# One mean product for the sum of squares before six stages of a two-block network kernel

## The chip, the cores and the metric

The kernel runs on one core of a Trainium2 chip. The metric is the device time of one execution in microseconds (us). Below, TensorE (PE in profile rows) multiplies matrices, VectorE (DVE) and ScalarE (ACT) work on tiles elementwise, and SyncE (SP) issues the loads. Each engine takes its instructions in the order in which the program wrote them and waits on semaphores for the others.

## The reference

A hybrid block of two layers is followed by a mixer block of one layer, on 512 tokens of width 1024, all in float32. Cut to what matters here, the norms and what stands on both sides of them:

```
def layer_norm(x, g, b):
    mu = xf.mean(-1);  var = square(xf - mu).mean(-1)
    return (xf - mu) * rsqrt(var + LN_EPS) * g + b
def rmsnorm(x, g):
    return x * rsqrt(mean(x * x, -1) + RMS_EPS) * g

# hybrid_layer, twice:
h = layer_norm(ALPHA * x + 0.5 * swiglu(x, ffn1_w_gu, ffn1_w_down), ...)
... = split(h @ w_in);  merged = gated sum of three branches
h = layer_norm(ALPHA * h + merged @ w_out, ...)
x = layer_norm(ALPHA * h + 0.5 * swiglu(h, ffn2_w_gu, ffn2_w_down), ...)
# second block, once:
x = x + token_mixer(rmsnorm(x, norm_mix_g), w_in, ..., w_out)
x = x + conv_ffn(rmsnorm(x, norm_ffn_g), w_up, ..., w_down)
return rmsnorm(x, norm_final_g)
```

Every `@` reduces over 1024 or more inputs, and every norm needs a mean of squares over the 1024 channels of each token.

## The kernel before, in words

**Tiles.** An activation is kept transposed: eight tiles of 128 channels by 512 tokens, R[0] to R[7] for the residual. Each matrix product is made of blocks of 128 by 128 weights. To hold float32 accuracy, a block is three products: the rounded weights by the rounded operand (L1982), the rounded weights by its rest (L1983), the rest of the weights by the rounded operand (L1991). Four blocks of weights arrive as one slab by DMA; ScalarE rounds the slab (L2253, `w_hi`) and VectorE makes its rest (L2606, `w_lo`).

**How a stage ends.** `update` makes the eight output tiles of `ffn1_down`, `w_out`, `ffn2_down` or their like in the second block. After tile m, VectorE adds it to the residual (`add_up`, L2624). ScalarE squares the tile (L2284, writes a page of SBUF), VectorE adds the squares of tiles up to m - 1 to a running total (`squares_add`, L2658), and in the layer norms it adds the tile itself to a running sum for the mean (L2671). A mean over channels, which lie on partitions, is a product with a 128 by 128 matrix whose entries are all 1/1024. It is a product in float32 of 128 by 512, which the trace shows as two records.

**How the next stage begins.** A norm's factors are known only once tile 7 is added up. So that TensorE needn't wait, the next stage begins its first products from the residual without its norm (class `Early`, in the text "early products"): ScalarE multiplies tile m by the gain and rounds it (L2332), VectorE makes the rest (L2682), and TensorE multiplies the eight tiles in their order; in layer norms it also multiplies the gains and offsets by the same weights (L1989, L1990, four columns wide). The norm is put right afterwards on the outputs. An `Early` has a `count` of such outputs: 2, except before the second block's mixer, where `EarlyTwice` has 4.

**The order around the change.** The order on each engine is set by one planner, which runs the program once with estimated times (`Pace`) and again identically for each engine. `stats.ended()` is where the norm of tile 7 is asked for: `behind(7)` is called there, behind the early part of tile 7 (L2332, L2682) and behind the early products of tiles 0 to 6 that the planner put ahead. `behind(7)` takes the total of the squares of tiles 0 to 6 and the squares of tile 7 apart: TensorE multiplies the first by the mean matrix (L2004), waits for the second, and adds its product to the same bank (L2007). In the layer norms one more product follows for the mean (`mean_matmul`, L1999), and then the square of the mean, the variance, its logarithm and an exponential (L2308, L2722, L2292, L2295). The products of tile 7 for the next stage come next on TensorE. In the second block's RMS norm there is no product for the mean.

`behind(7)` with L2004 and L2007 runs eight times: before the stages after `ffn1_down`, `w_out`, `ffn2_down` of layer 0, the same of layer 1, after `w_out_2`, and before the last norm.

Of the kernel before, what the change touches and what calls it, by code (L numbers as in the profile page):

```python
# [1596 lines left out]
class Squares:  # L1597
# [28 lines left out]
    def behind(self, m):  # L1626
        o, k = self.o, self.k
        while self.sq:
            t, q, squared = self.sq.pop(0)
            if not self.summed:  # L1630
                k.will(tensor="var")
                o.mean_matmul(k, self.v, q.f[:, :], self.first, t == 7, [squared])
                o.pages.give(q, k["var"])
            elif self.first:
                self.sum, k["sum"] = q, squared
            elif t < 7:
                before = k["sum"]
                k.will(vector="sum")
                o.squares_add(k, self.sum, q, before, squared)
                o.pages.give(q, k["sum"])  # L1640
            else:
                k.will(tensor="most var")
                o.mean_of_two(k, self.v, self.sum, q, squared)
                o.pages.give(self.sum, k["most"])
                o.pages.give(q, k["var"])
            self.first = False
# [1608 lines left out]
```

## Time and profile before

| | us |
|---|---|
| Median of 3 runs | 3683.18 |
| Lowest and highest run | 3682.66, 3684.90 |
| The profiled execution, its own time | 3684.97 |
| Its span, first to last instruction | 3683.2 |
| TensorE busy in it | 3628.9 |
| VectorE busy in it | 1978.8 |
| ScalarE busy in it | 1525.7 |

The page has the busy time of each engine, the span in 40 slices with the granted clock of TensorE, the chain of work that ended last, and groups of instructions. The busy time of TensorE says only that it seldom waits; what an edit is worth is read from the timeline at the place of the edit, where the start of each instruction, its duration and, in brackets, the idle time before it stand.

### The profile page before, as it was taken

To read this page: it belongs to the slowest core of one execution; us is meant where nothing else is said; L and a number is where in the kernel's file an instruction comes from. 1 tells how busy PE (TensorE), PEld (TensorE's weight loads), DVE (VectorE), ACT (ScalarE), POOL (GpSimd) and SP (SyncE) were. 2 spreads that over 40 slices of the span, in tenths; PEclk is the share of its full clock that TensorE was granted. 3 is DMA by queue.
4 is the path that set the end of the run, shared out by engine and by line. 5 is a ranking of instruction groups with operands and counts; after the bars stand their busy time and mean duration, and the time that the engine had idled before them with its cause. 6 is when DMAs were issued, how large, how long until landed. Compare 5 with 4: busy or idle time off the path is not lost.

```text
span 3683.2 us, 44504 instructions
## 1 busy us (share of the span) xinstructions
PE 3628.9 (99%) x17166; PEld 2913.6 (79%) x17166; DVE 1978.8 (54%) x3808; ACT 1525.7 (41%) x2928; POOL 0.2 (0%) x4
## 2 busy tenths in 40 slices
PE   9999999999999999999999999999998999999998
PEld 7888878877778888888888877788876677778887
DVE  4433565556753345334665576733346787566643
ACT  4433454454343334333554553533234444344432
POOL 0000000000000000000000000000000000000000
PEclk9999999999999999999999999999998999999999
DMA  4433321112333333333221113233322222233332
GB/s 147 120 112 94 87 86 52 44 47 71 90 87 94 94 95 88 93 94 94 86 66 49 43 56 87 84 94 94 94 72 64 82 65 82 82 89 94 94 94 89
DMA packets 169546, 308.42 MB, mean 84 GB/s; under 512 B 18870, under 2 KB 21079, under 8 KB 169336
## 3 DMA queue, kind: packets, MB, share of 16 engines
q1 hardware_dynamic: 169336, 305.59, 28.6%
q8 instruction: 136, 2.23, 0.3%
q14 instruction: 74, 0.61, 0.1%
HBM read 300.80 MB, written 4.72 MB: 83 GB/s over the span
## 4 chain that ended last, share of the span: by engine, by line
PE 93%; DVE 3%; ACT 2%; issue 1%; DMA 0%; DVEq 0%; SPq 0%; ACTq 0%
PE bank L1991 27%; PE bank L1982 27%; PE bank L1983 27%; PE bank L1965 3%; PE bank L2024 1%; PE bank L1970 1%; PE bank L1999 1%; PE bank L2044 1%; DVE w_lo L2606 1%; PE bank L2065 0%; PE bank L2199 0%; PE bank L2037 0%; PE bank L1990 0%; PE bank L2207 0%; DVE page_f L2677 0%
## 5 line engine op out<-in xcount | busy, mean ns | idle before, releaser
L1982 PE MATMUL bank<-page_r,w_hi 128*128 128x512 f32 (+1 forms) x4488 | 1803.3, 402 | 19.7 <-DVE w_lo L2606 11.3
L1991 PE MATMUL bank<-page_r,w_lo 128*128 128x512 f32 (+1 forms) x4488 | 1776.3, 396 | 0.0
L1983 PE MATMUL bank<-page_r,w_hi 128*128 128x512 f32 (+1 forms) x4488 | 1766.8, 394 | 0.0
L2253 ACT ACTIVATE w_hi<-raw 128x512 fp32r<-128x512 f32 x1122 | 699.0, 627 | 1024.4 <-PE bank L1991 1021.1
L1982 PEld LDWEIGHTS bank<-page_r,w_hi 128*128 128x128 f32 x4488 | 848.1, 189 | 225.6 <-issue 18.2
L1983 PEld LDWEIGHTS bank<-page_r,w_hi 128*128 128x128 f32 x4488 | 847.6, 189 | 192.2 <-issue 6.9
L1991 PEld LDWEIGHTS bank<-page_r,w_lo 128*128 128x128 f32 x4488 | 847.6, 189 | 192.1
L2606 DVE TENSOR_TENSOR w_lo<-raw,w_hi 128x512 fp32r<-128x512 f32 x1122 | 747.3, 687 | 438.4 <-ACT w_hi L2253 436.6
L2746 DVE TENSOR_TENSOR page_f<-page_f,bank 128x512 f32<-128x512 f32 x88 | 60.5, 688 | 321.8 <-PE bank L1991 275.3
L1965 PEld LDWEIGHTS bank<-page_f 128*128 128x128 f32 x1344 | 161.6, 192 | 9.1 <-issue 1.9
L1965 PE MATMUL bank<-page_f 128*128 128x128 f32 x1344 | 163.3, 276 | 0.4 <-DVE page_f L2940 0.4
L2624 DVE SCALAR_TENSOR_TENSOR page_f<-bank,page_f 128x512 f32<-128x512 f32 x64 | 44.2, 690 | 164.2 <-PE bank L1991 163.6
L2327 ACT ACTIVATE page_r<-page_f 128x512 fp32r<-128x512 f32 x88 | 55.6, 632 | 176.3 <-DVE page_f L2746 176.3
L2284 ACT ACTIVATE page_f<-page_f 128x512 f32<-128x512 f32 (+1 forms) x80 | 48.5, 611 | 147.2 <-DVE page_f L2624 131.1
L3074 DVE SCALAR_TENSOR_TENSOR page_f<-bank,par,page_f 128x511 f32<-128x511 f32 x88 | 65.4, 748 | 60.1 <-ACT page_f L2567 58.5
L2749 DVE TENSOR_TENSOR page_r<-page_f,page_r 128x512 fp32r<-128x512 f32 x88 | 60.9, 693 | 64.0 <-ACT page_r L2327 64.0
L2370 ACT ACTIVATE page_f<-bank 128x256 f32<-128x256 f32 (+3 forms) x144 | 50.2, 388 | 104.5 <-PE bank L1970 102.6
L1970 PE MATMUL bank<-cst,page_f 128*128 128x128 f32 x452 | 72.1, 277 | 4.9 <-DVE page_f L2898 2.9
L2360 ACT ACTIVATE page_f<-bank 128x512 f32<-128x512 f32 x80 | 47.7, 597 | 69.5 <-PE bank L1991 69.4
L2754 DVE SCALAR_TENSOR_TENSOR page_f<-page_f,bank 128x512 f32<-128x512 f32 x80 | 54.7, 685 | 39.0 <-PE bank L1991 38.7
L1970 PEld LDWEIGHTS bank<-cst,page_f 128*128 128x128 f32 x452 | 53.5, 141 | 25.3 <-issue 7.0
L2822 DVE SCALAR_TENSOR_TENSOR page_f<-bank,par,page_f 128x511 f32<-128x511 f32 (+2 forms) x72 | 53.8, 748 | 34.5 <-ACT page_f L2412 32.8
(235 smaller groups left out, 2394.5 us busy)
## 6 DMA issues: line engine op xcount, KB each, us to landing
raw<-weights SPq DMA_DIRECT2D x1122, 256.0 KB, 2.6
page_f<-x_t SPq DMA_DIRECT2D x8, 256.0 KB, 5.4
bias_rows<-page_f SPq DMA_DIRECT2D x8, 256.0 KB, 2.0
page_f<-bias_rows SPq DMA_DIRECT2D x8, 256.0 KB, 3.3
out_t<-page_f SPq DMA_DIRECT2D x8, 256.0 KB, 2.1
cst<-consts SPq DMA_DIRECT2D x4, 272.0 KB, 4.2
page_f<-mem_t SPq DMA_DIRECT2D x8, 128.0 KB, 3.3
bias_rows<-page_f SPq DMA_DIRECT2D x8, 64.0 KB, 1.9
```

What stands on the lines that cost most here:

```text
L1965: last = self.e.matmul(b.tile(i), x, y, start=True, stop=True)
L1970: last = self.e.transpose(b.tile(i), ap[:, i * P:(i + 1) * P], self.const("ident"))
L1982: self.e.matmul(o, hi, X.hi[kt], start=first, stop=False)
L1983: self.e.matmul(o, hi, X.lo[kt], start=False, stop=False)
L1991: last = self.e.matmul(o, lo, X.hi[kt], start=False, stop=final)
L2253: self.e.activation(self.m.w_hi[:, s % NHI, :], self.m.raw[:, s % NRAW, :], ACT.Copy) \
L2327: self.e.activation(h.r[:, :], s.f[:, :], ACT.Copy).then_inc(k.lane.scalar, 1)
L2606: self.e.tensor_tensor(self.m.w_lo[:, s % NRAW, :], self.m.raw[:, s % NRAW, :], self.m.w_hi[:, s % NHI, :].bitcast(F32), ALU.subtract).the ...
L2746: self.e.tensor_tensor(s.f[:, :], s.f[:, :], lift.f[:, :], ALU.mult).then_inc(k.lane.vector, 1)
L2749: self.e.tensor_tensor(l.r[:, :], s.f[:, :], h.r[:, :].bitcast(F32), ALU.subtract).then_inc(k.lane.vector, 1)
L2754: self.e.scalar_tensor_tensor(out=g.f[:, :], in0=g.f[:, :], scalar=1.0, in1=b.f[:, :], op0=ALU.add, op1=ALU.mult).then_inc(k.lane.vector, 1)
L3074: self.e.scalar_tensor_tensor(out=p.f[:, sh:], in0=b.f[:, 0:SEQ - sh], scalar=self.col("conv2", (2 - sh) * 2 * FT + m), in1=p.f[:, sh:], o ...
```

## The change

At the last tile, where the stage has an `Early` of two products, VectorE adds the squares of tile 7 to the total as well, and TensorE makes the mean with one product instead of two. The order in which two pages go back to the stock changes with it.

```
@@ Squares.behind
                 k.will(vector="sum")
                 o.squares_add(k, self.sum, q, before, squared)
                 o.pages.give(q, k["sum"])
+            elif self.early and self.early.count == 2:
+                before = k["sum"]
+                k.will(vector="sum", tensor="var")
+                o.squares_add(k, self.sum, q, before, squared)
+                o.mean_matmul(k, self.v, self.sum.f[:, :], True, True, [k["sum"]])
+                o.pages.give(q, k["sum"])
+                o.pages.give(self.sum, k["var"])
             else:
                 k.will(tensor="most var")
                 o.mean_of_two(k, self.v, self.sum, q, squared)
```

Six of the eight places have a count of 2: `ffn1_down`, `w_out` and `ffn2_down` of layer 0, `ffn1_down` and `w_out` of layer 1, and `w_out_2`. The one before the second block's mixer (a count of 4) and the last norm (no early products) stay. In all, TensorE has six products fewer and VectorE six additions more; ScalarE and SyncE have the same instructions in the same order. Lines of the changed kernel stand seven further down, so L2004 and L2007 give way to L2006, L2658 is L2665 and L2682 is L2689.

TensorE after `w_out` of layer 0, before the change (`cst` is the mean matrix, `page_f` squares or the sum of tiles, `page_r` and `w_hi` or `w_lo` an operand and weights):

```order
L1991 MATMUL bank<-page_r,w_lo 128x512
L2004 MATMUL bank<-page_f,cst 128x512 [waits norm_vector]
L2007 MATMUL bank<-page_f,cst 128x512 [waits norm_scalar]
L1999 MATMUL bank<-page_f,cst 128x512 [waits norm_vector]
L1982 MATMUL bank<-page_r,w_hi 128x512 [waits early_vector]
L1983 MATMUL bank<-page_r,w_hi 128x512
```

and with the change:

```order
L1998 MATMUL bank<-page_r,w_lo 128x512
L2006 MATMUL bank<-page_f,cst 128x512 [waits norm_vector]
L2006 MATMUL bank<-page_f,cst 128x512
L1989 MATMUL bank<-page_r,w_hi 128x512 [waits early_vector]
L1990 MATMUL bank<-page_r,w_hi 128x512
```

The product with the total that waited for the squares of tiles 0 to 6 and the one that waited for ScalarE's squares of tile 7 have become one, which waits for VectorE's new sum; the second L2006 is the product for the mean.

VectorE at the same place, before the change, from the addition of tile 7 on:

```order
L2624 SCALAR_TENSOR_TENSOR page_f<-bank,page_f 128x512 [waits norm_vector,blocks_multiplied]
L2671 TENSOR_TENSOR page_f<-page_f 128x512 [waits norm_vector]
L2682 SCALAR_TENSOR_TENSOR page_r<-page_f,par,page_r 128x512 [waits early_scalar]
L2722 TENSOR_TENSOR page_f<-bank,page_f 128x512 [waits norm_scalar,norm_tensor]
L2689 SCALAR_TENSOR_TENSOR page_f<-bank,page_f 128x512 [waits norm_scalar,norm_tensor,merge_vector]
```

and with the change:

```order
L2631 SCALAR_TENSOR_TENSOR page_f<-bank,page_f 128x512 [waits norm_vector,blocks_multiplied]
L2678 TENSOR_TENSOR page_f<-page_f 128x512 [waits norm_vector]
L2689 SCALAR_TENSOR_TENSOR page_r<-page_f,par,page_r 128x512 [waits early_scalar]
L2665 TENSOR_TENSOR page_f<-page_f 128x512 [waits norm_scalar]
L2729 TENSOR_TENSOR page_f<-bank,page_f 128x512 [waits norm_scalar,norm_tensor]
L2696 SCALAR_TENSOR_TENSOR page_f<-bank,page_f 128x512 [waits norm_scalar,norm_tensor,merge_vector]
```

The new addition (L2665) stands behind the rest of tile 7 (L2689, before L2682), which itself waits for ScalarE's rounding. At the other four places with a layer norm the rows are the same; after `w_out_2` the new addition stands between the rest of tile 7 and a slab's rest.

## Rows read from the trace of the kernel before

**Rows 1.** The page: busy times, granted clock in 40 slices, chain by engine.

```profile
PE 3628.9 (99%) x17166; PEld 2913.6 (79%) x17166; DVE 1978.8 (54%) x3808; ACT 1525.7 (41%) x2928; POOL 0.2 (0%) x4
PEclk9999999999999999999999999999998999999999
PE 93%; DVE 3%; ACT 2%; issue 1%; DMA 0%; DVEq 0%; SPq 0%; ACTq 0%
```

**Rows 2.** Timeline (start, duration, engine, line) after `ffn1_down` of layer 0.

```profile
431.61 0.63 ACT L2284 ACTIVATE page_f<-page_f 128x512 f32<-128x512 f32 x1 [2.83 <-DVE page_f L2624]
...
432.89 0.75 DVE L2682 SCALAR_TENSOR_TENSOR page_r<-page_f,par,page_r 128x512 fp32r<-128x512 f32 x1 [0.59 <-ACT page_r L2332]
...
433.44 1.02 PE L2004 MATMUL bank<-page_f,cst 128*128 128x512 f32 x2
...
435.15 1.02 PE L1999 MATMUL bank<-page_f,cst 128*128 128x512 f32 x2
...
436.25 0.40 PE L1983 MATMUL bank<-page_r,w_hi 128*128 128x512 f32 x1
...
436.91 0.69 DVE L2722 TENSOR_TENSOR page_f<-bank,page_f 128x512 f32<-128x512 f32 x1 [3.27 <-ACT page_f L2308]
```

**Rows 3.** The same after `ffn2_down` of layer 0.

```profile
1389.12 0.75 DVE L2682 SCALAR_TENSOR_TENSOR page_r<-page_f,par,page_r 128x512 fp32r<-128x512 f32 x1 [0.66 <-ACT page_r L2332]
...
1392.41 0.40 PE L1983 MATMUL bank<-page_r,w_hi 128*128 128x512 f32 x1
```

**Rows 4.** The same after `w_out` of layer 0.

```profile
1011.35 0.48 PE L1991 MATMUL bank<-page_r,w_lo 128*128 128x512 f32 x1
1011.76 0.69 DVE L2658 TENSOR_TENSOR page_f<-page_f 128x512 f32<-128x512 f32 x1
...
1012.50 1.13 PE L2004 MATMUL bank<-page_f,cst 128*128 128x512 f32 x2 [0.67 <-DVE page_f L2658]
...
1013.76 1.13 PE L2007 MATMUL bank<-page_f,cst 128*128 128x512 f32 x2
...
1014.36 0.75 DVE L2682 SCALAR_TENSOR_TENSOR page_r<-page_f,par,page_r 128x512 fp32r<-128x512 f32 x1 [0.58 <-ACT page_r L2332]
...
1014.73 1.02 PE L1999 MATMUL bank<-page_f,cst 128*128 128x512 f32 x2
...
1015.82 0.40 PE L1983 MATMUL bank<-page_r,w_hi 128*128 128x512 f32 x1
```

**Rows 5.** The same after `w_out_2`.

```profile
3301.92 0.75 DVE L2682 SCALAR_TENSOR_TENSOR page_r<-page_f,par,page_r 128x512 fp32r<-128x512 f32 x1 [1.31 <-ACT page_r L2332]
3302.59 0.69 DVE L2606 TENSOR_TENSOR w_lo<-raw,w_hi 128x512 fp32r<-128x512 f32 x1
...
3303.77 0.40 PE L1983 MATMUL bank<-page_r,w_hi 128*128 128x512 f32 x1
```

**Rows 6.** TensorE's timeline where it resumes after a wait (idle before in brackets).

```profile
662.49 3.35 PE L2065 MATMUL bank<-page_f,cst 128*128 128x512 f32 x4 [1.97 <-DVE page_f L2882]
...
666.07 0.54 PE L1983 MATMUL bank<-page_r,w_hi 128*128 128x512 f32 x1
...
1995.17 1.99 PE L2065 MATMUL bank<-page_f,cst 128*128 128x512 f32 x4 [1.99 <-DVE page_f L2882]
...
1997.22 0.40 PE L1983 MATMUL bank<-page_r,w_hi 128*128 128x512 f32 x1
...
2731.46 3.65 PE L1999 MATMUL bank<-page_f,cst 128*128 128x512 f32 x4 [3.56 <-ACT page_f L2284]
...
2767.27 0.77 PE L1982 MATMUL bank<-page_r,w_hi 128*128 128x512 f32 x1 [4.91 <-DVE page_r L2741]
```

**Rows 7.** TensorE by stretches: stretch, its length, busy (count), granted clock, DMA share, GB/s.

```profile
1016.00:1050.00 34.00, 34.00 (x160) 1.00 0.29 86
2730.00:2735.00 5.00, 3.54 (x5) 0.66 0.01 4
2765.00:2770.00 5.00, 2.73 (x7) 0.56 0.00 0
```

## The prediction

> **What bounds the kernel now.** I read the page first. TensorE is busy for 3628.9 of 3683.2 us, and the chain that ended last runs through it for 93% of the span [rows 1]. So what an edit is worth is what it does to TensorE's own sequence: a product taken away is a gain if TensorE isn't made to wait in its place, and work on VectorE (54% busy) costs nothing unless TensorE waits for its result. Both happen here in the same spot, so the busy shares decide nothing, and I went to the timeline at each of the six places. In each I take as goal the start of L1983 in the block of tile 7, the first ordinary product behind the mean products. The four things to look at are when TensorE reaches the first mean product, when the squares of tile 7 are ready, when VectorE ends the rest of tile 7 (L2682), and when L1983 starts.
>
> The sum is made against the profiled execution, whose span (3683.2 us) is almost equal to the median of the runs (3683.18), so I add the difference to the median.
>
> **What is removed.** One mean product of 128 by 512 in float32, six times. From L2004 to L1999 in rows 2 lie two of them: 435.15 - 433.44 = 1.71 us, so 0.86 us for one. Were nothing to wait, this would be 6 x 0.86 = 5.1 us gained.
>
> **What is added.** One VectorE addition of two 128x512 pages, and TensorE's wait for it. Its duration is that of the same operation on other squares, 0.69 us [rows 4]. Its start is set by its place behind L2682, because its other input is there early: after `ffn1_down` the squares are ready at 431.61 + 0.63 = 432.24, before L2682 even starts at 432.89 [rows 2]. Behind an L2682 the next VectorE instruction starts 3302.59 - 3301.92 = 0.67 us later [rows 5]. From the end of an addition to the product that waited for it are 1012.50 - (1011.76 + 0.69) = 0.05 us [rows 4]. So the one product now starts 0.67 + 0.69 + 0.05 = 1.41 us after the start of L2682. A mean product that TensorE had to wait for takes a little longer to the next: 1014.73 - 1013.76 = 0.97 us instead of 0.86 [rows 4]. From the mean's product L1999 to L1983 are 436.25 - 435.15 = 1.10 us [rows 2]. Thus with a layer norm L1983 starts 0.97 + 1.10 = 2.07 us behind the start of the one product.
>
> **Place by place.**
> - After `ffn1_down` of layer 0: one product at 432.89 + 1.41 = 434.30, L1983 at 436.37 in place of 436.25 [rows 2]: 0.12 us later. TensorE idles from 433.44 to 434.30, which is exactly the product that went away.
> - After `ffn2_down` of layer 0: 1389.12 + 1.41 + 2.07 = 1392.60 against 1392.41 [rows 3]: 0.19 later. `ffn1_down` of layer 1 repeats this pattern, another 0.17 to 0.19.
> - After `w_out` of layer 0: here VectorE is behind, because it still makes slab rests, and TensorE reaches the mean products before tile 7 is even added up. Before the change it uses the time: the total of tiles 0 to 6 is multiplied at 1012.50, tile 7's squares at 1013.76 [rows 4]. With the change it can do neither, and waits for L2682 and the addition: 1014.36 + 1.41 = 1015.77, then L1983 at 1017.84 against 1015.82 [rows 4]: 2.02 later. `w_out` of layer 1 is the same pattern, 2.02 again.
> - After `w_out_2`: no product for the mean, so L1983 comes 1.10 + 0.11 = 1.21 us behind the start of the one product (0.11 being what a product waited for takes longer). 3301.92 + 1.41 + 1.21 = 3304.54 against 3303.77 [rows 5]: 0.77 later.
>
> The sum: 0.12 + 2 x 0.18 + 2 x 2.02 + 0.77 = 5.3 us lost. The factors of the norm hang on the same mean products, so they come later by as much as TensorE does, and TensorE meets them at the same distance as before: nothing is given back and nothing is added. On VectorE the instruction behind the new addition waits for ScalarE and TensorE anyway (L2722 follows only when the mean's product is done), so there it covers nothing up. Only after `w_out_2` a slab's rest is pushed by one addition, and TensorE needs that slab three slabs later; I cost it at nothing, and at 0.7 us if that cover were gone. The swapped pages cost nothing, since ScalarE and SyncE keep their rows.
>
> **The clock.** After `w_out` TensorE will now stand still from 1011.35 + 0.48 = 1011.83 to 1015.77, 3.94 us, where the longest pause before was 0.67 us [rows 4] and the clock was granted in full (a 9 in every slice there, and 1.00 behind it) [rows 1, 7]. What such a pause does shows elsewhere. Behind one of 3.56 us the granted clock fell: 0.66 on average over 2730 to 2735. Behind one of 4.91 us it was 0.56 over 2765 to 2770 [rows 6, 7]. The levels being 1.2 and 2.4 GHz, that is most of each stretch at the lower one. Behind pauses of 2 us it is open: the same instructions took from L2065 to L1983 666.07 - 662.49 = 3.58 us in layer 0 and 1997.22 - 1995.17 = 2.05 in layer 1 [rows 6], so one fall costs 1.53 us and the other pause had none. 3.94 lies between the two long pauses, and I take a fall at both `w_out` places. Price: nothing at the low end; 1.7 us at the high end (the 0.66 over 5 us means 0.34 / 0.5 x 5 = 3.4 us at half the clock, and half of them are lost when all of them fall on work). In the stretch from 2765 on, 0.56 means 4.4 of 5 us at the lower level, while work resumed only at 2767.27: a part fell on the pause and cost nothing. So I take 1.35, between 0.7 and 1.7, twice: 2.7 us.
>
> The Trainium skill, in TensorE: Matmul & The Clock Gate, section "Why this matters for your kernels", says to leave no long idle gaps between bursts of matmuls, since one of them brings the lower clock back. That speaks against this change at the two `w_out` places; by this rule the sum is 8.0 us, and without it 5.3. The two long pauses of this trace agree with it.
>
> **Sum.** 5.3 + 2.7 = 8.0 us slower: 3683.2 + 8.0 = 3691.2 us, or 0.22%.
>
> **Rivals.**
> 1. The clock holds, or falls at one of the two places only. For: the twin pauses of 2 us went both ways. Against: both long ones fell. Time 5.3 to 6.9 us later, 3688.5 to 3690.1. Chance 0.24.
> 2. The loss is partly given back, because TensorE would later have waited for something that keeps its time, such as a weight load or VectorE's backlog. Against: TensorE is busy for all of the 34 us behind the first `w_out` place [rows 7], and the four other layer norm places look alike, so no wait is near that could swallow it. It would leave 0 to 4 us, 3683 to 3687. Chance 0.08.
> 3. Faster: the addition isn't late. If VectorE reaches it as soon as the squares are ready, TensorE doesn't wait at four of the places (all but the `w_out` ones) and keeps 0.86 us at each. It decides at the point where the addition ends before TensorE arrives: at 433.44 it would have to start by 432.70, before L2682 starts [rows 2]. The order puts it behind L2682, so this needs the layers' timing to shift. 3683.2 - 4 x 0.86 = 3679.8 at best if the `w_out` places lost nothing either. Chance 0.04.
> 4. VectorE becomes the bound behind the addition: 0.6 to 0.7 us more in its queue six times delays slab rests and the repair of the early products, up to 4 us on top, 3692 to 3695. Against: VectorE idled 3.27 us before L2722 [rows 2]. Chance 0.08.
>
> That the change doesn't do what it says is excluded by the order of the rows: six products fewer, six additions more, nothing else.
>
> **How the numbers follow.** The forecast (a fall at both places) has 0.56. Its own range is 5.3 + 2 x 0.7 = 6.7 to 5.3 + 2 x 1.7 = 8.7 us, so 3689.9 to 3691.9. The whole range takes in rival 1 and half of rival 4: 3687.2 to 3693.4. About 0.2% (7.4 us) is what a measurement of this kernel can tell from no change. Of the forecast's 0.56, three quarters lie beyond that (0.42), and with rival 4 slower has 0.50; same has 0.14 + 0.24 + 0.08 + half of rival 3, 0.47 together; faster 0.03.
>
> **What would show it.** In the profile after: at the three ffn places the one product L2006 preceded by 0.7 to 0.9 us of idle time, released by VectorE L2665, and L1990 (L1983 before) within 0.3 us of its old distance from the rest of tile 7; at the two `w_out` places 3.5 to 4 us of idle time before L2006, and a granted clock clearly under 1.00 in the 5 us behind; after `w_out_2` a wait for the addition as well. The step that I trust least is the price of the clock. If L2006 has no wait before it at the ffn places, the place of the addition was read wrongly; if the idle time is there and the end doesn't move, the view that nothing is given back is wrong.

## The result, and the profile after

| | before | after |
|---|---|---|
| Median, us | 3684.15 (9 runs) | 3694.45 (9 runs) |
| Lowest and highest run | 3682.66, 3685.19 | 3690.39, 3696.41 |
| Ratio, with its 95% interval | | 1.0026 [1.0016, 1.0035] |
| Profiled execution, its own time | 3684.97 | 3691.1 |
| Its span | 3683.2 | 3689.3 |

The change costs 10.3 us, 0.26%. The sign is the one forecast. The size is above the forecast (8.0 us) and the time is above the range (3693.4). The profiled execution lies near the low end of the runs of the changed kernel (3691.1, where the median is 3694.45), so sums made from its trace come out below the median.

The page of the changed kernel, beside [rows 1]: busy times, granted clock by slices, and the chain by engine.

```profile
PE 3628.6 (98%) x17154; PEld 2910.5 (79%) x17154; DVE 1982.5 (54%) x3814; ACT 1525.9 (41%) x2928; POOL 0.2 (0%) x4
PEclk9999999999999999999999999999998999999999
PE 94%; DVE 3%; ACT 2%; issue 1%; DMA 0%; DVEq 0%; ACTq 0%
```

TensorE has twelve records fewer (six products of two records) and still the same busy time. So what the six products saved, some 5 us, came back as longer products elsewhere, and the longer span is idle time on top. A digit of the clock row shows neither: a slice is 92 us long, and a fall of a few microseconds doesn't change it. The waits of TensorE name the new idle time (what it waited for: us in all, times, longest):

```profile
PE bank L2006 <- DVE page_f L2665: 8.4, 6, 2.4
```

Now the six places. After `ffn1_down` of layer 0, beside [rows 2] (start, duration, engine, line, idle before in brackets):

```profile
432.17 0.75 DVE L2689 SCALAR_TENSOR_TENSOR page_r<-page_f,par,page_r 128x512 fp32r<-128x512 f32 x1 [0.59 <-ACT page_r L2339]
...
432.84 0.68 DVE L2665 TENSOR_TENSOR page_f<-page_f 128x512 f32<-128x512 f32 x1
...
433.58 1.98 PE L2006 MATMUL bank<-page_f,cst 128*128 128x512 f32 x4 [0.70 <-DVE page_f L2665]
...
435.63 0.39 PE L1990 MATMUL bank<-page_r,w_hi 128*128 128x512 f32 x1
```

From the rest of tile 7 (L2689) to the one product are 433.58 - 432.17 = 1.41 us, and from there to L1990 2.05. The prediction had 1.41 and 2.07. After `ffn2_down` of layer 0, beside [rows 3]:

```profile
1390.49 0.75 DVE L2689 SCALAR_TENSOR_TENSOR page_r<-page_f,par,page_r 128x512 fp32r<-128x512 f32 x1 [0.66 <-ACT page_r L2339]
...
1391.90 1.98 PE L2006 MATMUL bank<-page_f,cst 128*128 128x512 f32 x4 [0.77 <-DVE page_f L2665]
1393.95 0.39 PE L1990 MATMUL bank<-page_r,w_hi 128*128 128x512 f32 x1
```

L1990 stands 3.46 us behind L2689, where it was 3.29. After `w_out_2`, beside [rows 5], 3309.91 - 3307.31 = 2.60 us in place of 1.85, so 0.75 lost where 0.77 was predicted:

```profile
3307.31 0.75 DVE L2689 SCALAR_TENSOR_TENSOR page_r<-page_f,par,page_r 128x512 fp32r<-128x512 f32 x1 [1.31 <-ACT page_r L2339]
3307.98 0.68 DVE L2665 TENSOR_TENSOR page_f<-page_f 128x512 f32<-128x512 f32 x1
...
3308.72 1.12 PE L2006 MATMUL bank<-page_f,cst 128*128 128x512 f32 x2 [1.36 <-DVE page_f L2665]
...
3309.91 0.39 PE L1990 MATMUL bank<-page_r,w_hi 128*128 128x512 f32 x1
```

And after `w_out` of layer 0, beside [rows 4]: TensorE and VectorE.

```profile
1010.60 0.48 PE L1998 MATMUL bank<-page_r,w_lo 128*128 128x512 f32 x1
1013.48 3.63 PE L2006 MATMUL bank<-page_f,cst 128*128 128x512 f32 x4 [2.40 <-DVE page_f L2665]
1016.27 1.07 PE L1989 MATMUL bank<-page_r,w_hi 128*128 128x512 f32 x1
1017.18 0.40 PE L1990 MATMUL bank<-page_r,w_hi 128*128 128x512 f32 x1
...
1012.07 0.75 DVE L2689 SCALAR_TENSOR_TENSOR page_r<-page_f,par,page_r 128x512 fp32r<-128x512 f32 x1 [0.58 <-ACT page_r L2339]
1012.74 0.68 DVE L2665 TENSOR_TENSOR page_f<-page_f 128x512 f32<-128x512 f32 x1
```

Two things differ from the prediction here. The pause is 2.40 us, not 3.94. And the two products L2006 take 3.63 us for what took 1.98 at the ffn places: from the one product to L1990 are 3.70 us, not 2.05. The windows say why. TensorE by stretches: stretch, its length, busy (count), granted clock, DMA share, GB/s; the changed kernel:

```profile
990.00:1000.00 10.00, 7.99 (x29) 0.83 0.17 55
1010.00:1025.00 15.00, 12.60 (x55) 0.89 0.15 47
2325.00:2335.00 10.00, 8.00 (x28) 0.83 0.20 54
2345.00:2360.00 15.00, 12.58 (x55) 0.89 0.13 41
```

The clock fell behind the pause at both `w_out` places, as forecast, and also 20 us earlier, behind an old pause of 2.0 us in which TensorE waits for a slab's rest:

```profile
992.50 0.50 PE L1989 MATMUL bank<-page_r,w_hi 128*128 128x512 f32 x1 [2.01 <-DVE w_lo L2613]
992.84 0.54 PE L1990 MATMUL bank<-page_r,w_hi 128*128 128x512 f32 x1
993.18 0.63 PE L1998 MATMUL bank<-page_r,w_lo 128*128 128x512 f32 x1
```

**How I cut the traces.** Two executions of one kernel differ by 1 or 2 us at pauses that the change doesn't touch, so starts in one trace can't be set against starts in another. Distances between two marks can. As marks I take the resumption behind that 2.0 us pause (L1982 before, L1989 after) and VectorE's addition of tile 7 after `ffn2_down` (L2624, L2631). Between them lies one `w_out` place and nothing else of the change. In the kernel before they are

```profile
994.79 0.50 PE L1982 MATMUL bank<-page_r,w_hi 128*128 128x512 f32 x1 [2.01 <-DVE w_lo L2606]
...
1387.05 0.69 DVE L2624 SCALAR_TENSOR_TENSOR page_f<-bank,page_f 128x512 f32<-128x512 f32 x1 [2.98 <-PE bank L1991]
```

and after, from 992.50 above to

```profile
1388.41 0.69 DVE L2631 SCALAR_TENSOR_TENSOR page_f<-bank,page_f 128x512 f32<-128x512 f32 x1 [2.98 <-PE bank L1998]
```

so 392.26 us before and 395.91 after: 3.65 us for this place. Cutting the whole program in this way (marks read from the timelines; 662 and 1995 stand for the product behind two other old pauses of 2 us, L2065 before and L2072 after; 2731 for the product behind the 3.56 us pause):

| stretch | before | after | difference | predicted |
|---|---|---|---|---|
| start to 662 | 662.49 | 661.91 | -0.58 | 0.12 |
| 662 to the pause ahead of `w_out` | 332.30 | 330.59 | -1.71 | |
| `w_out` of layer 0 | 392.26 | 395.91 | +3.65 | 2.02 + 1.35 |
| to 1995 (two ffn places) | 608.12 | 608.44 | +0.32 | 0.36 |
| 1995 to the pause ahead of `w_out` | 330.56 | 330.52 | -0.04 | |
| `w_out` of layer 1 | 392.26 | 395.79 | +3.53 | 2.02 + 1.35 |
| to 2731 | 13.47 | 13.49 | +0.02 | |
| to L1990 after `w_out_2` | 572.31 | 573.26 | +0.95 | 0.77 |
| to the end | 379.4 | 379.4 | 0.0 | |

The first ffn place costs 0.10 us (5.46 us from the addition of tile 7 to L1990, before 5.36). Of the 0.95 in the stretch of `w_out_2`, 0.75 is the place itself, so the six places of the change sum to 0.10 + 3.65 + 0.32 + 3.53 + 0.75 = 8.35 us. The other 0.2 of that stretch is what two changes of the clock leave over: it stayed low for a shorter time behind 2827 (from 2731 to the resumption at 3258.86 are 527.40 us, and 526.26 after), and it fell behind a pause of 1.57 us at 3262.91 (granted 0.83 over 3260 to 3270, where it had been 1.00 behind the same pause). The -1.71 is a fall of the clock behind the pause at 662, which this execution of the kernel before had [rows 6] and this one of the changed kernel had not; executions of both kernels without that fall are met below, so it isn't put down to the change. It is the main reason why the spans differ by 6.1 us only.

### The profile page after: what moved, and what is told of

It is laid out like the page before. It is cut to its first block, busy times and chain, and to the rows that moved or that the text cites. A ratio compares the mean times of both kernels' runs of the same rounds, so it can differ in the third digit from the quotient of the medians.

```text
span 3689.3 us, 44487 instructions
## 1 busy us (share of the span) xinstructions
PE 3628.6 (98%) x17154; PEld 2910.5 (79%) x17154; DVE 1982.5 (54%) x3814; ACT 1525.9 (41%) x2928; POOL 0.2 (0%) x4
## 4 chain that ended last, share of the span: by engine, by line
PE 94%; DVE 3%; ACT 2%; issue 1%; DMA 0%; DVEq 0%; ACTq 0%
PE bank L1989 27%; PE bank L1998 27%; PE bank L1990 27%; PE bank L1972 3%; PE bank L2031 1%; PE bank L1977 1%; PE bank L2006 1%; PE bank L2051 1%; PE bank L2206 0%; PE bank L2072 0%; PE bank L2044 0%; DVE w_lo L2613 0%; ACT page_r L2339 0%; PE bank L1997 0%; PE bank L2214 0%
## 5 line engine op out<-in xcount | busy, mean ns | idle before, releaser
L1989 PE MATMUL bank<-page_r,w_hi 128*128 128x512 f32 (+1 forms) x4488 | 1801.9, 402 | 19.4 <-DVE w_lo L2613 11.0
L1990 PE MATMUL bank<-page_r,w_hi 128*128 128x512 f32 (+1 forms) x4488 | 1765.0, 393 | 0.0
L1989 PEld LDWEIGHTS bank<-page_r,w_hi 128*128 128x128 f32 x4488 | 847.8, 189 | 226.7 <-issue 19.5
L1990 PEld LDWEIGHTS bank<-page_r,w_hi 128*128 128x128 f32 x4488 | 847.3, 189 | 193.7 <-issue 7.0
L2631 DVE SCALAR_TENSOR_TENSOR page_f<-bank,page_f 128x512 f32<-128x512 f32 x64 | 44.2, 691 | 165.4 <-PE bank L1998 164.8
```

The costliest lines, as they stand in the source:

```text
L1989: self.e.matmul(o, hi, X.hi[kt], start=first, stop=False)
L1990: self.e.matmul(o, hi, X.lo[kt], start=False, stop=False)
```

## The experiments

In the diffs, a removed line is one of the changed kernel unless a sentence says otherwise. `self.early.number` is the number of the layer norm, 0 to 5; 1 and 4 are those behind `w_out` of the two layers.

**The change alone at its two kinds of place, once more in full, and with the pause filled.** `again` is the changed kernel. `wout_only` keeps the change at the two `w_out` places, `others_only` at the four others:

```diff
-            elif self.early and self.early.count == 2:
+            elif self.early and self.early.number in (1, 4):                               # wout_only
+            elif self.early and self.early.count == 2 and self.early.number not in (1, 4): # others_only
```

`fill` is the changed kernel with three float32 products of constants ahead of the waiting product at the two `w_out` places. They go to the bank that the mean product then overwrites, so what is computed stays the same.

```diff
             elif self.early and self.early.count == 2:
...
+                if self.early.number in (1, 4):
+                    o.fill(self.v, 3)
...
+    def fill(self, v, n):
+        self.clear(v)
+        for _ in range(n):
+            self.e.matmul(v.cols(SEQ), self.const("mean"), self.m.cst[:, 0:SEQ], start=True, stop=True)
```

> The changed kernel once more, for a second profile. Theory A (the loss is TensorE's longer wait at the two w_out places plus the lower clock that such a pause brings): the runs scatter over several us, since the pause falls differently on the clock each time; a pause of 2.4 to 4.0 us before L2006 at both w_out places, a granted clock under 1.00 behind each. Rival B (the additions push VectorE's later work at all six places): the same time with little scatter, and new waits of TensorE elsewhere. Time 10 us over the kernel before, within 2 us, by both.

> The change at the two w_out places alone, the other four as before. Theory A: nearly all of the loss, 7 to 10 us over the kernel before. Rival B (each addition costs its own length and a slab's delay, wherever it stands): a third of it, about 3.4 us.

> The change at the four other places alone, the two w_out places as before. Theory A: 0.12 + 2 x 0.18 + 0.77 = 1.3 us over the kernel before, and no fall of the clock behind L2006. Rival B: two thirds of the loss, about 7 us.

> The changed kernel with three idle products (mean matrix by constants, 0.86 us each) issued at each w_out place before the product that waits for the addition; their result is overwritten. They change no dependence, they only keep TensorE working for 2.6 us of the pause. Theory A: the clock stays full behind the w_out places and the time is what is left without the clock's part, 5 to 6 us over the kernel before, some 4 to 5 us under the changed kernel. Rival B (the clock doesn't matter, VectorE does): no change against the changed kernel, 10 us.

| | median, us | against before | ratio |
|---|---|---|---|
| again | 3693.01 | +8.8 | 1.0023 [1.0015, 1.0032] |
| wout_only | 3691.92 | +7.7 | 1.0024 [1.0014, 1.0033] |
| others_only | 3683.84 | -0.3 | 1.0000 [0.9991, 1.0009] |
| fill | 3690.28 | +6.1 | 1.0017 [1.0008, 1.0026] |

The loss belongs to the two `w_out` places. At the four others the trace of the changed kernel has 0.70 + 0.77 + 0.75 + 1.36 = 3.6 us of idle time before L2006, against four products of 0.86 saved; what is left, 1.3 us by the prediction, is too small for the runs to find. (In the trace of `others_only` the two ffn places between the marks cost 608.44 - 608.12 = 0.32 us again.) `fill` parts the two halves of the loss at `w_out`. Its median is 2.7 us under that of `again`, where 4 to 5 had been expected, and the intervals of the two overlap; the split rests on the distances in its trace. TensorE around the second of these places, and the windows:

```profile
2343.95 2.73 PE L2013 MATMUL bank<-cst 128*128 128x512 f32 x6
...
2348.05 1.98 PE L2008 MATMUL bank<-page_f,cst 128*128 128x512 f32 x4 [1.36 <-DVE page_f L2672]
...
2350.10 0.40 PE L1992 MATMUL bank<-page_r,w_hi 128*128 128x512 f32 x1
```

```profile
1010.00:1025.00 15.00, 15.00 (x70) 1.00 0.15 41
...
2345.00:2360.00 15.00, 13.63 (x63) 1.00 0.16 41
```

With TensorE at work in most of the pause the clock stays at its upper level (1.00), and from the product to L1992 are again 2.05 us. The distance over the `w_out` place is now 394.26 us in layer 0 (992.23 to 1386.49) and 394.25 in layer 1: 2.00 and 1.99 us more than before the change, where the prediction's wait was 2.02. So the wait costs 2.0 us per place. What the changed kernel loses above that goes with the clock: the same products and the same wait, without the fall, don't have it.

**The addition earlier.** In `first_four`, VectorE adds the squares of tile 7 before it makes the rest of tile 7 (only the order on VectorE changes); the two `w_out` places are as in the kernel before. `first_all` does the same at all six places.

```diff
     def tile(self, m):
...
+        if m == 7 and self.early and self.early.count == 2:      # first_four: and number not in (1, 4)
+            t, q, squared = self.sq.pop(0)
+            before = self.k["sum"]
+            self.k.will(vector="sum")
+            o.squares_add(self.k, self.sum, q, before, squared)
+            o.pages.give(q, self.k["sum"])
+            self.added = True
         if self.early:
             self.early.tile(m)
...
-            elif self.early and self.early.count == 2:
+            elif self.early and False:                          # the order of the changed kernel is off
...
         self.behind(7)
+        if self.added:
+            self.k.will(tensor="var")
+            self.o.mean_matmul(self.k, self.v, self.sum.f[:, :], True, True, [self.k["sum"]])
```

`again2` and `again3` are the changed kernel in one profiled execution each, since its runs spread more (3690 to 3696) than those of the kernel before.

> At the four places other than w_out VectorE adds tile 7's squares between the running sum (or the residual's addition) and the rest of tile 7, where it sat idle for 0.59 us (1.31 after w_out_2) waiting for ScalarE; one mean product. The two w_out places as in the kernel before. Theory A (what costs is that the addition stands behind the rest, so that TensorE waits): the addition ends before TensorE arrives, no wait before the mean product, and 4 x 0.86 = 3.4 us are gained against the kernel before, less 0.1 us at each place where the rest of tile 7 starts later. Rival (any addition in VectorE's queue at this point costs what the product saves): no gain, within 0.5 us of the kernel before.

> The same early addition at all six places. At w_out TensorE still waits for it, but from 1011.8 to about 1014.5 instead of 1015.8: Theory A: 0.75 us lost at each w_out place by the wait (2.07 us behind 1014.5 against 1015.82), and a pause of 2.7 us, behind which the clock falls in some executions; so 2 to 5 us slower than the version with four places, 0 to 2 us from the kernel before, 7 to 9 us under the changed kernel. Rival: as slow as the changed kernel at w_out, since the pause alone decides.

> The changed kernel in another execution, to see the pause and the clock at the w_out places again. Two profiles so far both had a fall of the clock at 992 us, a pause of 2.4 us at w_out and another fall. Theory A: without a fall at 992 us the pause is 3.9 us and the clock is lower for longer behind it, for a total of 8 to 12 us over the kernel before. Rival: every execution looks like the two seen, and the runs over 3693 us lose their time elsewhere.

> The same as the run before it, for one more execution: Theory A: pause before L2006 at w_out and the falls of the clock around it add up to the difference from the kernel before within 1 us. Rival: a part over 1 us lies elsewhere.

`first_four` took 3682.08 us, 2.0 less than before, 0.9994 [0.9985, 1.0003]. `first_all` took 3685.37, 1.3 more, 1.0005 [0.9996, 1.0014]. Neither interval excludes the kernel before; the distances do. In `first_four` the stretch with two ffn places is 606.39 us (1385.45 to 1991.84), 1.73 less than the 608.12 before and 2.05 less than the 608.44 of the changed kernel: one product per place, as expected. So VectorE's order was the reason for the loss at the ffn places. At `w_out` the addition is late even when it stands first: `first_all` still has there

```profile
PE bank L2018 <- DVE page_f L2677: 5.3, 2, 2.7
```

and its distance over the place is 394.63 and 394.66 us, 2.4 more than before, with a clock of 0.89 behind it (19.70 us from the resumption to L2018 and 2.05 to L2002 would be 0.7 us of wait; the rest is slower products). By the distances `first_all` should be 4.8 us behind `first_four`; the medians differ by 3.3 us, which the intervals (some 3 us to either side of each) don't part from 4.8.

`again2` and `again3` took 3695.63 and 3696.38 us. In layer 0 they show the case that I had predicted and that the first profile hadn't: no fall behind the old 2.0 us pause, and then the full pause at `w_out`. (In layer 1 both had the fall at 2332 and the short pause, 2.46 and 2.42 us.) TensorE in `again3`, and its windows:

```profile
1011.62 0.48 PE L1998 MATMUL bank<-page_r,w_lo 128*128 128x512 f32 x1
1016.04 3.78 PE L2006 MATMUL bank<-page_f,cst 128*128 128x512 f32 x4 [3.94 <-DVE page_f L2665]
1018.84 1.42 PE L1989 MATMUL bank<-page_r,w_hi 128*128 128x512 f32 x1
1020.05 0.63 PE L1990 MATMUL bank<-page_r,w_hi 128*128 128x512 f32 x1
...
1020.76 0.77 PE L1998 MATMUL bank<-page_r,w_lo 128*128 128x512 f32 x1
```

```profile
990.00:1000.00 10.00, 7.99 (x35) 1.00 0.26 79
1010.00:1025.00 15.00, 11.06 (x39) 0.77 0.11 35
```

The pause is 3.94 us, to the hundredth what was predicted. The clock behind it is 0.77 over 15 us, against 0.89 in the first profile: (1 - 0.77) / 0.5 x 15 = 6.9 us at the lower level instead of 3.3. The products are still slow behind L1990. With the marks as above (995.07 to 1392.24) this place costs 397.17 - 392.26 = 4.91 us.

Why is the pause 2.40 us in one execution and 3.94 in another? VectorE comes to the new addition at the same distance from the resumption ahead of it: 1012.74 - 992.50 = 20.24 us in the first profile, 1015.30 - 995.07 = 20.23 in `again3`. It is TensorE that comes later in the first, because its clock had fallen on the way: it ends its last early product 18.58 us behind the resumption instead of 17.03. So a fall at 993 costs next to nothing by itself (VectorE is the one waited for) and shortens the pause by as much. A second execution of the kernel before (`before2`) has the same: it had a fall at 992 (0.83), and the distance over `w_out` was 392.42 us, 0.16 more.

The cost of a `w_out` place in the four profiles of the changed kernel, from the same marks:

| | layer 0 | layer 1 |
|---|---|---|
| the first profile | 3.65 | 3.53 |
| again | 3.39 | 3.41 |
| again2 | 4.74 | 3.40 |
| again3 | 4.91 | 3.52 |

Take the wait of 2.02 off, and the clock cost 1.4 to 1.6 us where it was at the lower level for some 3.3 us, and 2.7 to 2.9 where it was there twice as long.

The `w_out` places are only a part of what sets the longer executions of the changed kernel apart, so the expectation for `again3`, that they make up the difference from the kernel before within 1 us, fell. The profiled span of `again3` is 6.2 us longer than that of `again`, and the `w_out` places differ by 1.6. The falls behind the old pauses at 662 and 2000 make up 3.2: `again2` and `again3` had both (granted 0.89 over 15 us), `again` and the first profile neither (1.00), and the stretches to the next pause are 332.26 and 332.09 us in `again3`, 330.59 and 330.55 in `again`. The other 1.3 lie ahead of 662. The kernel before had one of these two falls in each of its two profiles.

**One more place, and the old pauses.** `first_five` is `first_four` with the second block's mixer added (`number not in (1, 4)` alone, so its early products of a count of 4 too). `kept_clock` is the kernel before with idle products like those of `fill` in the old pauses; `best` is the two together; `before2` is the kernel before in one more execution.

```diff
+IDLE_BLOCKS = {3408: 5}
...
+            if self.next_block in IDLE_BLOCKS:
...
+                self.fill(b, IDLE_BLOCKS[self.next_block])      # ahead of block 3408, which waits 4.9 us
...
+                if self.first:
+                    o.fill(self.v, 4)                           # ahead of the mixer norm's first product
...
+        self.units = getattr(self, "units", -1) + 1
+        if self.units % 8 == 0:
+            self.fill(b, 2)                                     # twice, ahead of a unit's sum
...
+        if not getattr(self, "scored", False):
+            self.scored = True
+            self.fill(b, 6)                                     # ahead of the second block's first scores
```

> The early addition at the four places other than w_out and also before the second block's mixer (the place with a count of 4). Theory A: another 0.86 us less the 0.1 us by which the rest of tile 7 starts later, about 3 us under the kernel before in all; no wait before the mean product at the five places. Rival: as the kernel before within 0.5 us.

> The kernel before with idle products (0.86 us each, overwritten) in its own long pauses: 2 in each of the two of 2.0 us at 662 and 1995 us, 4 in that of 3.6 us at 2728, 5 in that of 4.9 us at 2762, 6 in that of 5.3 us at 2798. Nothing else is changed. Theory A (the lower clock behind a pause is the price, and keeping TensorE at work avoids it): 1.7 us back at 2731, up to 2 us behind 2767, up to 2 us behind 2804, 1.7 us at one of the 2 us pauses, so 4 to 7 us under the kernel before. Rival (the clock goes by something else than the pause): no gain, or a loss of 1 us where the idle products end after the wait.

> first_five and kept_clock together: the sum of the two, 7 to 10 us under the kernel before by theory A; by the rivals within 1 us of it.

> The kernel before in another execution, for a second profile: which of its pauses of 2 us (at 661, 993, 1993, 2324) are followed by a lower clock this time. Theory A: one to three of them, not the same as in the first, at 1.5 to 1.7 us each, while the pause before L2004 at w_out stays under 1 us and has none. Rival: the same falls as in the first profile.

`first_five` took 3682.36 us, 1.9 less than before, 0.9996 [0.9987, 1.0005]: the fifth place adds nothing that the runs can tell. In its trace the stretch of that place is 12.63 us (2714.92 to 2727.55) instead of 13.47, one product less. Its timeline after `ffn1_down` of layer 0 shows what the change could have been:

```profile
431.29 0.63 ACT L2303 ACTIVATE page_f<-page_f 128x512 f32<-128x512 f32 x1 [2.84 <-DVE page_f L2643]
...
431.96 0.69 DVE L2677 TENSOR_TENSOR page_f<-page_f 128x512 f32<-128x512 f32 x1
...
432.57 0.75 DVE L2701 SCALAR_TENSOR_TENSOR page_r<-page_f,par,page_r 128x512 fp32r<-128x512 f32 x1
...
433.12 1.88 PE L2018 MATMUL bank<-page_f,cst 128*128 128x512 f32 x4
...
435.07 0.39 PE L2002 MATMUL bank<-page_r,w_hi 128*128 128x512 f32 x1
```

The addition fits into the gap in which VectorE waited for ScalarE's rounding: the rest (L2701) has no idle time before it now, and TensorE has no wait before L2018. From ScalarE's squaring to L2002 are 3.78 us, before 436.25 - 431.61 = 4.64 [rows 2]: one product, 0.86, is gained.

`kept_clock` took 3684.62 us, no gain where 4 to 7 us had been expected, with two clusters of runs (3677.8 to 3679.2 and 3684.6 to 3685.6). In its profile the two fills ahead of the unit sums stood where TensorE wasn't pausing, and cost 1.7 us each (233.32 us from the addition of tile 7 to the product behind the pause at 662, before 231.61). That was a wrong choice of place. The profiled execution, 3679.21 us, is of the faster cluster and also had a full clock over 2815 to 2840, where the kernel before had 0.80 over 2820 to 2845; whether that parts the two clusters isn't shown. `best` took 3678.17, 0.9986 [0.9977, 0.9995], 6.1 us less than before, where 7 to 10 had been expected. `before2` took 3683.79; it is the second execution used above.

**What was still open.** `spare_add` is the kernel before with VectorE's extra addition at the six places, into a page that nothing reads, and TensorE left alone. `kept2` and `best2` are `kept_clock` and `best` without the two misplaced fills.

```diff
                 k.will(tensor="most var")
                 o.mean_of_two(k, self.v, self.sum, q, squared)
+                if self.early and self.early.count == 2:        # spare_add, against the kernel before
+                    spare = o.pages.take()
+                    k.will(vector="spare")
+                    o.spare_add(k, spare, q, squared)
+                    o.pages.give(spare, k["spare"])
...
-        self.units = getattr(self, "units", -1) + 1             # kept2 and best2,
-        if self.units % 8 == 0:                                 # against kept_clock and best
-            self.fill(b, 2)
```

> The kernel before with one more VectorE addition of 128x512 at the six places, at the same position as in the changed kernel, into a page that nobody reads; TensorE's products are as before. Theory A (the wait and the clock behind it are the whole loss): within 0.5 us of the kernel before. Rival B (the addition delays VectorE's later work, which TensorE then waits for): 2 to 4 us slower.

> The kernel before with idle products only in its three long pauses (4 at 2728, 5 at 2762, 6 at 2798 us). Theory A: the falls of the clock behind them go in most executions, 3 to 6 us under the kernel before, with two clusters of times if a fall still comes in some. Rival: as the kernel before.

> first_five with those three sets of idle products: Theory A: 3681.2 expected of first_five (3 us under the kernel before) less 3 to 6 us, so 3675 to 3678 us. Rival: as first_five.

| | median, us | against before | ratio |
|---|---|---|---|
| spare_add | 3684.40 | +0.4 | 1.0000 [0.9991, 1.0009] |
| kept2 | 3681.00 | -3.0 | 0.9989 [0.9981, 0.9998] |
| best2 | 3677.53 | -6.5 | 0.9982 [0.9973, 0.9991] |

The six additions alone cost nothing that the runs can tell, and in the trace of `spare_add` the stretch with two of them is 608.13 us (1384.41 to 1992.54) against 608.12. The fills do what they should; the granted clock over the three old long pauses, first before, then `kept2`:

```profile
2725.00:2735.00 10.00, 6.44 (x21) 0.83 0.17 53
2760.00:2770.00 10.00, 5.09 (x18) 0.78 0.08 26
2797.00:2812.00 15.00, 9.66 (x41) 0.66 0.01 2
```

```profile
2725.00:2735.00 10.00, 9.66 (x33) 1.00 0.07 27
2760.00:2770.00 10.00, 9.13 (x32) 1.00 0.10 31
2797.00:2812.00 15.00, 14.86 (x69) 1.00 0.18 44
```

In `kept2` the first waiting product still starts 13.47 us behind the addition of tile 7, as before, so the fill ahead of it cost nothing there. `best2` beats both kernels: 6.5 us faster than before and, by the differences of the two from the kernel before, 15 us or more faster than the changed one. It has five fewer products to make the means and 15 idle ones.

## Why the prediction was right or wrong

**What is removed, what is added: right.** The distances of 1.41 us (rest to product) and 2.07 us (product to L1983) came out as 1.41 and 2.05 at every ffn place. At these places the idle time before L2006 is 0.70 to 0.77 us, and the products saved are eaten by it. `others_only` finds no difference, `spare_add` finds that the additions themselves cost nothing.

**The wait at `w_out`: right in what it costs.** 2.02 us per place; `fill` measured 2.00 and 1.99. The predicted start of the one product, 1015.77 - 994.79 = 20.98 us behind the resumption, is 20.98 in the first profile and 20.97 in `again3`. The length of the pause was right only in two of eight cases: I had taken TensorE's arrival from one execution and overlooked that it depends on the clock behind the old 2.0 us pause ahead of it. In the other six the pause was 2.4 to 2.5 us.

**Nothing is given back: right.** In the table of stretches no stretch behind a place is shorter than before by more than 0.04 us, but for the 1.1 us of clock named below the table. Rival 2 falls.

**The clock: right in kind, too small in size.** This is the step that failed, and the one that the prediction trusted least. It forecast a fall at both places and took 1.35 us each, with 1.7 as the upper bound, where 1.7 stood for 3.4 us at the lower level with all of it on work. Neither the 1.35 nor the 0.7 below it was worked out from a row. In the profiles of the changed kernel the eight cases cost 3.82 us on average with the wait, so 1.8 for the clock, and up to 2.9. The upper bound was wrong because it rested on one length, read behind one old pause: behind the full pause of 3.94 us the lower level held twice as long. The trace of the kernel before had shown as much. I had read the window behind the 4.91 us pause up to 2770 only; up to 2775 it is

```profile
2765.00:2775.00 10.00, 7.73 (x23) 0.66 0.09 26
```

which is (1 - 0.66) / 0.5 x 10 = 6.8 us at the lower level in place of the 4.4 that I counted. At least 4.5 of them fall on work behind the resumption at 2767.27, so by the prediction's own way of pricing this row alone gives 2.3 us or more. Rival 1 (no fall, or one) falls: every profile has both.

**The sum again.** With 3.82 in place of 3.37 per place it is 1.25 + 2 x 3.82 = 8.9 us, which is the 8.8 that `again` measured. The comparison at the top had 10.3; its interval, 1.0016 to 1.0035, is 5.9 to 12.9 us, so both fit. Against the forecast of 3691.2, three things add up: 0.9 us from the clock, 1.0 us because the median of the three runs shown (3683.18) lay below that of the nine (3684.15), and the rest (3694.45 - 3691.2 = 3.25, so 1.35) is the spread of a kernel whose falls differ from one execution to the next. The range had no term for the last two. The profiles show what such a spread is made of, 1.5 to 1.7 us for each fall behind the old pauses at 662 and 2000, but four profiles don't tell how often each comes, so the 1.35 can't be put down to them with certainty. Without the last two terms the time would have been inside the range: 3683.2 + 8.9 = 3692.1 us.

**Rival 3 (faster) fell for the stated reason:** the order puts the addition behind the rest of tile 7, and no timing shifted that. But its mechanism is real: with the addition first, an ffn place gains its 0.86 us in the traces (`first_four`, `first_five`). The runs, at 2.0 and 1.9 us less than before, can't tell this from no change by themselves. **Rival 4** (VectorE becomes the bound) falls by `spare_add`. (The chances of same and faster add up to 0.48 and 0.02, not to 0.47 and 0.03.)

## What to carry over

A product moved from one engine to an addition on another is paid at the place where its result is waited for: write down, place by place, which engine arrives last there, and leave out the places where the receiving engine is the late one. Put the new instruction into a gap of that engine rather than behind its next job. If TensorE will pause, price the slower clock behind it from several executions, since the same place can cost 1.4 or 2.9 us on top of its wait, and try filling the pause with products whose results are thrown away.

## What the runs showed of the hardware

- A pause of 2.0 us was followed by a lower clock in some executions and not in others of the same kernel (at 992 in `before2`, not in the first profile of the kernel before). Pauses of 2.40 to 3.94 us at `w_out` were followed by one in all profiles. Behind 3.94 us the lower level held for some 6.9 us in `again3`, twice as long as behind 2.40. Shorter pauses can have it too: behind 1.57 us the clock was 0.83 over 10 us in the first profile of the changed kernel, and 1.00 behind the same pause in the kernel before.
- The length of a fall isn't set by the pause alone: behind the 3.56 us pause the clock was 0.89 over 15 us in the kernel before and 0.77 in `fill`, whose instructions there are the same. Nor does every fall follow a pause: over 2827 to 2840 of the kernel before it was 0.61 while TensorE was busy for all of the 13 us, and it had been 1.00, with TensorE busy throughout, over 2813 to 2827. Four-column products (L2215, L2217) had begun at 2823; that they are the cause isn't shown.
- A fall costs little where another engine is the one waited for: 392.42 us with a fall at 992, 392.26 without. It shortens the next pause.
- Idle float32 products in a pause kept the granted clock at 1.00 at all five pauses that were filled (`fill`, `kept2`). Where they stand inside the pause they cost nothing that shows (`kept2`: 3.0 us gained with 15 of them); where TensorE has work, two of them cost 1.7 us.
- Over stretches of 392 us without a fall of the clock, layers and executions of one kernel agree to 0.01 us (392.26, 392.26, 392.25). That is what makes distances between marks in a trace far sharper than the times of whole runs, which spread by 2 us and more.
